# RWKV-7 + sparse attention step: tokens first in the opening, and a new order of small pieces in the recurrence

## The reference, cut to what matters

```python
c_act = jax.nn.silu(c)
sh1, sc1, gt1, sh2, sc2, gt2 = jnp.split(c_act @ P['ada_w'][l] + P['ada_b'][l], 6, axis=-1)   # "modulation"
h = modulate(rms_norm(x, P['norm_mix_g'][l]), sh1, sc1)
...
def step(s, inp):                                   # wkv7_scan, s: matrix state of a head, 64 x 64
    r_t, w_t, k_t, v_t, a_t, b_t = inp
    sa = jnp.einsum('bhij,bhj->bhi', s, a_t)
    s = s * w_t[:, :, None, :] + sa[..., None] * b_t[:, :, None, :] + v_t[..., None] * k_t[:, :, None, :]
    return s, jnp.einsum('bhij,bhj->bhi', s, r_t)
...
mu = jnp.mean(y, axis=-1, keepdims=True)            # y: what the scan returned, centred here
var = jnp.mean(jnp.square(y - mu), axis=-1, keepdims=True)
yn = ((y - mu) * lax.rsqrt(var + LNX_EPS)).reshape(B, T, C) * P['rwkv_lnx_w'][l] + P['rwkv_lnx_b'][l]
```

## Time and profile before

| what | value |
|---|---|
| median of 3 runs | 1934.34 us (1934.26 to 1943.77) |
| profiled execution, its own time | 1931.51 us |
| its span in the trace | 1929.7 us |
| mean granted TensorE clock | 0.977 |
| TensorE busy | 1797.7 us, 93% |
| VectorE, ScalarE, GpSimd busy | 671.5, 510.6, 100.1 us |
| opening, to the first r, k, v product | 0 to 47 us |
| recurrence, iterations 0 to 9 | 274 to 680 us |

### The profile page before, as it was taken

The page is one execution under the profiler, slowest core; times in us unless marked ns, Lnnn a source line. Parts: engine busy times, 40 slices in busy tenths (PEclk is TensorE's granted clock), DMA queues, the critical chain, the costliest instruction groups (busy, mean ns, idle before and its releaser), DMA issues.

```text
span 1929.7 us, 52708 instructions
## 1 busy us (share of the span) xinstructions
PE 1797.7 (93%) x23279; PEld 1445.7 (75%) x23279; DVE 671.5 (35%) x1804; ACT 510.6 (26%) x1215; POOL 100.1 (5%) x155
## 2 busy tenths in 40 slices
PE   4999999998988898999999899999999989999997
PEld 3776777777776677899988764587777778999984
DVE  5240125666664333111012310304888232111104
ACT  2112223333331122111112210313887231111103
POOL 2111100000000002000001000000000001000002
PEclk9999999999999998999999899898999999999998
DMA  8565745333333488999987993354000287999944
GB/s 304 172 236 187 262 132 166 102 101 108 114 115 121 159 228 312 356 411 416 417 334 222 202 232 120 122 134 121 2 2 2 57 360 261 411 413 417 416 162 162
DMA packets 195382, 413.48 MB, mean 214 GB/s; under 512 B 53686, under 2 KB 135314, under 8 KB 186674
## 3 DMA queue, kind: packets, MB, share of 16 engines
q1 hardware_dynamic: 176386, 357.95, 54.0%
q0 software_dynamic: 11040, 39.85, 5.7%
q10 hardware_dynamic: 7760, 12.79, 1.9%
HBM read 356.84 MB, written 57.91 MB: 215 GB/s over the span
## 4 chain that ended last, share of the span: by engine, by line
PE 45%; issue 7%; DVE 5%; DMA 2%; ACT 1%; DVEq 1%; POOL 0%; ACTq 0%; SPq 0%
PE bank L2002 12%; PE bank L1997 6%; PE bank L2015 5%; PE bank L2021 4%; PE bank L1724 3%; PE bank L2881 3%; PE bank L2991 1%; PE bank L1990 1%; PE bank L3026 1%; PE bank L1979 1%; DMA region_b<-in_cmp_w_dram 1%; PE bank L2938 1%; PE bank L2102 1%; DVE region_a L3292 1%; PE bank L2813 1%
## 5 line engine op out<-in xcount | busy, mean ns | idle before, releaser
L1997 PE MATMUL bank<-wu,slot_x 128*32 128x384 f32 x1056 | 122.5, 497 | 4.5 <-issue 4.5
L1997 PE MATMUL bank<-wg,slot_x 128*32 128x384 f32 x1056 | 119.7, 493 | 3.8 <-ACT slot_x L2191 2.4
L2002 PE MATMUL bank<-wu,slot_x 128*32 128x128 f32 x1056 | 122.6, 277 | 0.0
L2002 PE MATMUL bank<-wg,slot_x 128*32 128x128 f32 x1056 | 121.1, 275 | 0.0
L2002 PEld LDWEIGHTS bank<-wu,slot_x 128*32 128x32 f32 x1056 | 117.4, 113 | 3.0
L2015 PE MATMUL bank<-wd,actT 128*32 128x384 f32 x1056 | 117.5, 486 | 1.3 <-ACT actT L2214 1.3
L2021 PE MATMUL bank<-wd,actT 128*32 128x256 f32 (+1 forms) x704 | 118.1, 326 | 0.0
L2002 PEld LDWEIGHTS bank<-wg,slot_x 128*32 128x32 f32 x1056 | 114.6, 111 | 0.4
L640 PE MATMUL bank<-xm,wp 128*128 128x272 f32 x480 | 113.3, 395 | 0.0
L640 PEld LDWEIGHTS bank<-xm,wp 128*128 128x128 f32 x480 | 90.4, 190 | 20.5 <-issue 2.7
L2427 DVE TENSOR_TENSOR act<-bank,act 128x384 f32<-128x384 f32 x32 | 17.9, 558 | 249.8 <-PE bank L2002 249.8
(11 more groups left out here) (646 smaller groups left out, 4012.5 us busy)
## 6 DMA issues: line engine op xcount, KB each, us to landing
wg<-in_moe_w_gate_dram SPq DMA_DIRECT2D x22, 2048.0 KB, 11.4
wu<-in_moe_w_up_dram SPq DMA_DIRECT2D x22, 2048.0 KB, 16.1
wd<-in_moe_w_down_dram SPq DMA_DIRECT2D x22, 2048.0 KB, 11.5
xT<-in_ada_w_dram SPq DMA_DIRECT2D x40, 1024.0 KB, 6.0
w<-in_moe_w_gate_dram SPq DMA_DIRECT2D x10, 2048.0 KB, 11.6
fT<-in_moe_w_up_dram SPq DMA_DIRECT2D x10, 2048.0 KB, 16.2
gall<-in_moe_w_down_dram SPq DMA_DIRECT2D x10, 2048.0 KB, 11.2
wp<-in_rwkv_w_rkv_dram SPq DMA_DIRECT2D x24, 512.0 KB, 4.6
```

Of the source, the lines that this page charges most:

```text
L1997: mm = pe.matmul(ps[32 * j:32 * j + 32, 0:GW], x[:, k, 32 * j:32 * j + 32], w[:, k, 0:GW], start=k == 0, stop=k == KT - 1)
L2002: mm = pe.matmul(ps[96:128, q * 128:(q + 1) * 128], x[:, kk, 32 * q:32 * q + 32], w[:, kk, GW:FF], start=kk == 0, stop=kk == KT - 1)
```

## The change

- Opening: TensorE waits for the tokens alone and turns them first (nine groups, banks 0 to 7 and 0 again), then waits for the vectors and turns these into banks 2 and 3. The squares start after the ninth eviction; silu(c) moves behind the squares on ScalarE; pe_norm_sum stands ahead of the waits for silu(c) and for the vectors' evictions.
- VectorE's centring stands first in stage 0.
- The modulation's quarter 0 moves ahead of the turns of k and b in stage 4, quarter 3 from stage 6 to stage 7, ahead of the states that come in. Quarters 1 and 2 stay.
- Sample states 4 to 7 (bank 7) are turned before the wait for pair_done, the other four behind it as before.

```diff
@@ TensorE, opening
             pe.wait_ge(S("pool_made"), 1)
+            pe.wait_ge(S("x_loaded"), 32)
+            for g in range(9):
+                if g >= 8:
+                    pe.wait_ge(S("in_ev"), g - 7)
...
             pe.wait_ge(S("vec_loaded"), 16 * 17)
+            pe.wait_ge(S("in_ev"), 3)
             for g in range(4):
                 rows = (72, 64, 128, 24)[g]
-                mm = pe.transpose(bank[0][:, g * 128:g * 128 + rows], B.vs[0:rows, g, :], ident[0:rows, 0:rows])
+                mm = pe.transpose(bank[2][:, g * 128:g * 128 + rows], B.vs[0:rows, g, :], ident[0:rows, 0:rows])
             mm.then_inc(S("in_tr"), 1)
-            pe.transpose(bank[1][:, 0:112], B.vs[0:112, 4, :], ident[0:112, 0:112]).then_inc(S("in_tr"), 1)
-            pe.wait_ge(S("x_loaded"), 32)
-            for g in range(2, 11):
...
+            pe.wait_ge(S("in_ev"), 4)
+            pe.transpose(bank[3][:, 0:112], B.vs[0:112, 4, :], ident[0:112, 0:112]).then_inc(S("in_tr"), 1)
+
+            pe_norm_sum(pe, B, 0)
             pe.wait_ge(S("cact_ready"), 1)
             pe.wait_ge(S("in_ev"), 11)
-
-            pe_norm_sum(pe, B, 0)
@@ act_norm
-        act.wait_ge(S("x_ready"), n) if n else act.wait_ge(S("in_ev"), 11)
+        act.wait_ge(S("x_ready"), n) if n else act.wait_ge(S("in_ev"), 9)
...
+    if n == 0:
+        act.wait_ge(S("in_ev"), 10)
+        act.activation(B.cact[:, :, 0:NC].rearrange("p k n -> p n k"), B.vT[:, 0, 0:72].rearrange("p (n k) -> p n k", k=KT), ACT.Silu)\
+           .then_inc(S("cact_ready"), 1)
@@ pe_rwkv
             if s == 7:
+                pe_late_vector(pe, B, it, 3)
                 pe_states_in(pe, B, a)
...
-            if s == 6:
-                pe_late_vector(pe, B, it, 3)
+            if s == 4:
+                pe_late_vector(pe, B, it, 0)
             if s != 5:
                 pe_first(pe, B, a, c, d, s)
...
-            if 4 <= s <= 5:
-                pe_late_vector(pe, B, it, 2 * s - 8)
+            if s == 5:
+                pe_late_vector(pe, B, it, 2)
@@ dve_rwkv
-            if 0 <= d < PAIRS and s == 5:
+            if 0 <= d < PAIRS and s in (0, 5):
                 dve_tail(dve, B, d, s)
...
-            if 0 <= d < PAIRS and s != 5:
+            if 0 <= d < PAIRS and s not in (0, 5):
                 dve_tail(dve, B, d, s)
@@ pe_second
     if s == 7:
+        if 0 <= b < PAIRS:
+            pe.wait_ge(S("samp_ev"), 8 * (b + 1))
+            for i in range(4, DB):
+                pe.transpose(bank[7][0:HD, at(i % 4, 128)], B.STs[b % 2][:, i], ident[:])
         if 0 <= d < PAIRS:
             pe.wait_ge(S("pair_done"), d + 1)
...
         if 0 <= b < PAIRS:
-            pe.wait_ge(S("samp_ev"), 8 * (b + 1))
-            for i in range(DB):
-                mm = pe.transpose(bank[6 + i // 4][0:HD, at(i % 4, 128)], B.STs[b % 2][:, i], ident[:])
+            for i in range(4):
+                mm = pe.transpose(bank[6][0:HD, at(i, 128)], B.STs[b % 2][:, i], ident[:])
             mm.then_inc(S("st_out_s_mm"), 1)
```

More of the change, by code:

```diff
@@ L379, in _ @@
             pe.wait_ge(S("pool_made"), 1)
+            pe.wait_ge(S("x_loaded"), 32)
+            for g in range(9):
+                if g >= 8:
+                    pe.wait_ge(S("in_ev"), g - 7)
+                if g < 8:
+                    t, h = g // 2, g % 2
+                    for q in range(4):
+                        k = 4 * h + q
+                        mm = pe.transpose(bank[g][:, q * 128:(q + 1) * 128], B.xt[:, t, k * 128:(k + 1) * 128], ident[:])
+                else:
+                    for k in range(KT):
+                        mm = pe.transpose(bank[0][:, k * NS:(k + 1) * NS], B.xt[0:NS, 4, k * 128:(k + 1) * 128],
+                                          ident[0:NS, 0:NS])
+                mm.then_inc(S("in_tr"), 1)
             pe.wait_ge(S("vec_loaded"), 16 * 17)
+            pe.wait_ge(S("in_ev"), 3)
             for g in range(4):
                 rows = (72, 64, 128, 24)[g]
-                mm = pe.transpose(bank[0][:, g * 128:g * 128 + rows], B.vs[0:rows, g, :], ident[0:rows, 0:rows])
+                mm = pe.transpose(bank[2][:, g * 128:g * 128 + rows], B.vs[0:rows, g, :], ident[0:rows, 0:rows])
             mm.then_inc(S("in_tr"), 1)
-            pe.transpose(bank[1][:, 0:112], B.vs[0:112, 4, :], ident[0:112, 0:112]).then_inc(S("in_tr"), 1)
-            pe.wait_ge(S("x_loaded"), 32)
-            for g in range(2, 11):
[L388 to L399, removed]
+            pe.wait_ge(S("in_ev"), 4)
+            pe.transpose(bank[3][:, 0:112], B.vs[0:112, 4, :], ident[0:112, 0:112]).then_inc(S("in_tr"), 1)
+            pe_norm_sum(pe, B, 0)
             pe.wait_ge(S("cact_ready"), 1)
             pe.wait_ge(S("in_ev"), 11)
-            pe_norm_sum(pe, B, 0)
             for j in range(ADA_FIRST):
@@ L530, in _ @@
         def _(dve):
+            dve.memset(B.cact[:], 0.0)
             for g in range(11):
                 dve.wait_ge(S("in_tr"), g + 1)
-                if g == 0:
-                    dve.memset(B.cact[:], 0.0)
+                if g < 8:
+                    t, h = g // 2, g % 2
+                    ins = dve.tensor_copy(B.xT[:, 4 * h:4 * h + 4, t * 128:(t + 1) * 128],
+                                          bank[g][:].rearrange("p (k n) -> p k n", k=4))
+                elif g == 8:
+                    ins = dve.tensor_copy(B.xT[:, :, SEQ:T], bank[0][:, 0:KT * NS].rearrange("p (k n) -> p k n", k=KT))
+                elif g == 9:
                     dve.drain()
@@ L537, in _ @@
                         rows = (72, 64, 128, 24)[q]
[L538 to L544, removed]
+                        ins = dve.tensor_copy(B.vT[:, q, 0:rows], bank[2][:, q * 128:q * 128 + rows])
                 else:
-                    ins = dve.tensor_copy(B.xT[:, :, SEQ:T], bank[g % 8][:, 0:KT * NS].rearrange("p (k n) -> p k n", k=KT))
+                    ins = dve.tensor_copy(B.vT[:, 4, 0:112], bank[3][:, 0:112])
                 ins.then_inc(S("in_ev"), 1)
+            dve.drain()
             dve.wait_ge(S("pool_made"), 2)
```

3 lines of the change are left out of this document (removed).

## The result

The changed kernel took 1906.01 us (median of 4 runs, 1904.78 to 1910.01), the kernel before in the same comparison 1936.48 us (4 runs, 1934.26 to 1943.77): a ratio of 0.9844, 95% interval 0.9813 to 0.9874. That is faster by 1.6%, 30 us, where 20.8 were forecast.

A forecast was written before the change was run, and what follows sets the result against it. TensorE's order with its waits was taken as the bound, in opening and recurrence. Opening -6.4 and recurrence -14.4 (-26.5 filled, +12.1 bared) gave -20.8: 1934.3 to 1913.5 us, range 1905 to 1923, likeliest case's own range 1907 to 1920.

The forecast's parts named there:

- The opening: Opening: tokens turned at 11.4 instead of 17.51, squares and what follows 6.4 us earlier; bounds 0 and 6.7.
- Step 1, centring: Recurrence, VectorE's centring in its idle time: TensorE's 6.6 us wait for the chain ending in L1364 falls by 3.2.
- Step 2, chunks: Recurrence, quarter 0 ahead of L1036 also stands ahead of the awaited chunk: 4.0 of 4.9 us go.
- Step 3, weights: Recurrence, quarters' weight loads start earlier: of 14.5 us waits 3.5 stay, in iterations 7, 8 and 0, so -11.0.
- Step 4, states: Recurrence, quarter 3 in stage 7 covers the 0.74 us wait before the states come in: -5.2.
- Step 5, sample states: Recurrence, four sample states turned before pair_done fill about 0.5 us of a 0.9 wait, six iterations: -3.1.
- What was left bare: Recurrence, new waits: first Gram product +4.5, third +6.7 (7.7 less 1.0 waited before), row copy +0.9; sum +12.1 us.
- The recurrence gives nothing: Rival: ScalarE's bared evictions cost what the fills save, only the opening's gain is left: 1928 us; chance 0.12.
- The opening gives nothing: Rival: weights or VectorE set the first r, k, v product at 47.44 after all: 1920 us; chance 0.06.
- Table switches: Rival, opening on ScalarE: from 1.8 us a switch instead of 1.3, two make the root late: 1915; chance 0.03.
- Slower by the clock: Rival, recurrence: new 1.5 us waits bring more low-clock stretches of 1.7 us, slower from 18 on: 1954; chance 0.04.
- More than the sum: Rival, recurrence: shorter wait spares the half-clock quarter at 621.43, some 3 us, perhaps another 1.7: 1909; chance 0.05.

The follow-up runs named there:

- recurrence alone: Kernel before with only the centring first, quarters 0 and 3 moved and four sample states early: 1917.43 us, ratio 0.9929.
- before, again: Kernel before, unchanged, run once more for a second trace: 1936.72 us, ratio 1.0013.
- opening alone: Kernel before with only the opening's edits: 1927.53 us, ratio 0.9970.
- changed, again: Changed kernel, no edit, run once more for a second trace: 1911.31 us, ratio 0.9903.
- changed, quarter 0 behind: Changed kernel with quarter 0 moved behind the turns of k and b and the samples, ahead of the chunk: iteration 44.8 us, no whole time given.
- changed, tail first: Changed kernel with ScalarE evicting the tail's turn ahead of the inverse's eviction in stage 6: 1903.82 us, ratio 0.9851.
- changed, both: Changed kernel with the tail evicted before the inverse in stage 6 and quarter 0 behind turns and samples: 1908.39 us, ratio 0.9843.

## Why the prediction was right, and where its numbers were off

**The opening.** -6.4 forecast, -6.40 in the trace. Two errors in it cancelled. The samples' load landed at 10.6, not 11.4, and the turns started 0.65 earlier than forecast; but they took 5.44 us instead of 4.82, since TensorE's first products are slow and more of them were tokens' turns than before (last section). That the second decimal agrees is luck: the first r, k, v product comes at 46.55 to 49.15 in the seven traces with the old opening and at 40.46 to 42.68 in the six with the new one, and the means, 47.4 and 41.4, lie 6.0 apart. The slack of 0.3 at the eighth quarter was in truth missing (wait 0.49), at no cost, as argued: VectorE's scaling ended later. The table loads cost 1.30 a switch and no drain is to be seen. The Trainium skill's figure (ScalarE: Activation LUTs, "What ACT_TABLE_LOAD costs"), 2.66 us for every switch, would have added 1.7 us by the prediction's estimate; it does not hold here, and the measurement decides.

**Step 1, centring.** Six waits of 0.57 forecast, 3.4; measured 3.8, five of 0.55 to 0.57 and one of 0.94. **Step 2, chunks.** 4.0 of 4.9 to go; 0.9 left (in the list: two waits above a tenth each). **Step 3, weights.** 3.5 to stay; 3.8 stayed (2.4 and 1.4), though not where forecast: 1.4, 1.0 and 1.4 in iterations 7, 8 and 0, where 2.1, 0.6 and 0.8 were taken. **Step 4, states.** 5.2 to 0, and so it came. **Step 5, sample states.** 3.1 of 6.2 to go; 3.3 went.

**What was left bare.** First Gram product 4.5 forecast, 4.8 measured; third 7.7 forecast, 7.7 measured; row copy 0.9 forecast, 1.5 or more measured: the two iterations without states waited 0.73 each, and the six others 0.09 where none were taken. Missing in the prediction was the inverse's last stage: in iterations 0, 1 and 7, which have no tail or no preparation, quarter 3 had also covered VectorE's and ScalarE's step before it, and 1.4 us lie bare there.

**The sum.** The recurrence was to give 14.4. The traces show 12.7 between first inverse and output projection, the recurrence alone gave 15.5 in time (13.7 by the ratio). The clock has no part in the missing 1.7: the two traces spend 11.1 and 11.2 us of this stretch at half clock. TensorE's idle time there tells where the forecast was high:

| kernel | idle us, first inverse to output projection |
|---|---|
| order as before: before, again, opening alone | 48.7, 46.9, 49.1 |
| centring alone | 44.7 |
| sample states alone | 44.2 |
| both quarters alone | 42.9 |
| quarter 3 alone | 47.4 |
| all three: changed, again, recurrence alone | 36.0, 35.9, 35.8 |
| changed, quarter 0 behind | 36.7 |
| changed, tail first | 31.3 |
| changed, both | 30.7 |

Against the mean of 48.2 the centring wins 3.5 where 3.2 were forecast, the sample states 4.0 (3.1), the quarters 5.3, where their terms (-4.0 - 11.0 - 5.2 + 12.1) give 8.1. Values of one order lie up to 2 us apart, and only the last is off by more than that: the waits that the quarters left bare, the inverse's last stage among them, cost more than was taken. Together the three win 12.3, and singly 12.8, so they hardly disturb one another. In an iteration at full clock the waits came out as forecast (4.7 to 3.2), and the busy time was 0.3 us shorter, which was not foreseen: 44.8 instead of 45.1.

**The size.** The measured 30 us are outside the likeliest case's own range, which ended at 1907, and inside the stated one. The term that was off is the last one of the sum: all behind the recurrence carried over unchanged. It was 7.6 us shorter in the trace, 5.7 of them by the wait for compression weights and what followed it, which came back in the second trace. The median of the kernel before was also 2.1 us higher in this comparison than the 1934.3 from which the forecast started. At the same mean clock 19 to 22 us lie between the kernels, and the second comparison gave 21.6. What decides how much half clock an execution gets stays open. The prediction had priced such stretches only as a danger (18 of them for "slower") and not as a spread of 6 to 9 us on every median, which the three times of before, 1934.26 to 1943.77, could have told.

**The rivals.** The recurrence gives nothing: out, it gave two thirds. The opening gives nothing: out. Table switches: out. Slower by the clock: the new waits of 1.5 us brought no more of it in the recurrence; it has two and six stretches in the traces of the kernel before, two and one in those of the changed kernel, four with the opening alone and four with the recurrence alone. More than the sum: the stretch is spared, the gain is not there. In iteration 7, where the quarters' waits went from 1.7 to 3.5 us down to 0.9 to 1.8, a half-clock stretch begins in all six traces with quarter 0 in its old place and in none of the seven others. In four of the six it begins ahead of the wait, so the wait is not shown to be its cause. And other stretches came (iterations 0 and 8 of the changed kernel), and the time at half clock in the recurrence stayed the same.

## What to carry to other kernels

Where one engine's list of small pieces is the bound, write its waits down for one period with what ends each, and treat a movable piece as a plug: its worth is the wait that it fills less the wait that it uncovers, plus what its own loads gain or lose by the new distance. A piece whose removal uncovers a wait may point at a cheaper cure: here the order of two evictions on ScalarE was worth 1.3 us in iterations 2 to 4, where all three of the recurrence's edits together brought 1.8. Look at every period all the same, for in iterations 5 and 6 little of it was left (4.6 us in all, against 12.7). Judge such edits by an undisturbed period and by TensorE's idle time over the whole stretch; the whole time spread more from run to run than any of them was worth.

## What the runs showed of the hardware that was not expected

- TensorE's first products are slow although the window view shows full clock. In the changed kernel groups of four turns start 0.85 us apart until 14.19 and 0.44 from 14.71 on; in the kernel before 0.85 until 19.21 and 0.44 from 19.98 on, so fewer of its tokens' turns were slow. The record of the granted clock begins only at 14.36 and at 19.87, where the pace changes; ahead of that the view's 1.00 is no measurement. The two paces stand to each other like the two levels, 1.2 and 2.4 GHz. The Trainium skill (TensorE: Matmul & The Clock Gate, "What's actually happening") has 1.2 GHz as the state before any work, and the traces agree. In the view of windows eight turns of the changed kernel go through in 1.70 us at first, and sixteen later:

```profile
10.75:12.45 1.70, 1.70 (x8) 1.70 (x9) 0.58 (x1) 0.00 (x0) 1.50 (x3) 1.00 1.04 371
14.40:16.10 1.70, 1.70 (x16) 1.55 (x15) 1.67 (x3) 0.00 (x0) 0.00 (x0) 1.00 1.04 411
```

- Executions of one program on one core differ by up to 21 us (7 runs of the kernel before, 1923.76 to 1945.16), and the spans go with the mean clock, 1.7 us for each 0.001. In the thirteen traces a wait of 4.6 to 6.0 us for a load was missing once, with nothing changed near it.
- With the quarters moved, TensorE's busy time in iterations 2 to 4 was 0.3 us shorter (of 41.9) for the same instructions, and these iterations got shorter by it. Over the whole recurrence nothing of it is left (356.88 and 356.92 us). Whether this is the hardware or how the ends of overlapping products are modelled stays open.
